# Making 56 modulation tiles during the projections of the mixing sublayers instead of in the 768-token FFNs

## The reference

```python
c_act = jax.nn.silu(c); cc_act = jax.nn.silu(c_ctx)
for layer in range(DEPTH):                                    # DEPTH = 2
    mod   = (c_act @ w_mod[layer] + b_mod[layer])             # 9 vectors of 1024
    mod_c = (cc_act @ w_mod[layer] + b_mod[layer])
    x, xc = hybrid_layer(x, xc, mod, mod_c, ...)
def ffn_sublayer(h, m, sub, ...):                             # shift, scale, gate = 3 of the 9
    y = swiglu(modulate(rms_norm(h, g_pre[sub]), shift, scale), w1, w2)
    return h + MACARON_WEIGHT * gate * rms_norm(y, g_post[sub])
```

## Time and profile before

| | |
|---|---|
| median of 3 runs | 3765.51 us (3759.2 to 3771.49) |
| the profiled execution | 3757.21 us, span 3755.4 us |
| TensorE busy | 3530.5 us, 94% |
| VectorE busy | 2183.8 us, 58% |
| ScalarE, GpSimd busy | 1434.2 us, 721.5 us |
| mean granted TensorE clock | 0.966 |

### The profile page before, as it was taken

The page is one execution under the profiler, slowest core; times in us unless marked ns, Lnnn a source line. Parts: engine busy times, 40 slices in busy tenths (PEclk is TensorE's granted clock), DMA queues, the critical chain, the costliest instruction groups (busy, mean ns, idle before and its releaser), DMA issues.

```text
span 3755.4 us, 52062 instructions
## 1 busy us (share of the span) xinstructions
PE 3530.5 (94%) x19855; PEld 3030.4 (81%) x19855; DVE 2183.8 (58%) x3395; ACT 1434.2 (38%) x2510; POOL 721.5 (19%) x299
## 2 busy tenths in 40 slices
PE   6899999988999999999999898899998999899998
PEld 4899997856789999789999676788878898589656
DVE  6888875167488888788887429421226462541134
ACT  4433333157353333543334317432234423221353
POOL 1111112200211111211111220244442232034202
PEclk9999999999999999999999998999998999799899
DMA  6333332110233332433333220123332222022101
GB/s 227 107 124 123 124 120 86 62 36 1 91 118 116 121 117 97 157 109 116 113 113 119 82 70 17 46 90 100 96 95 68 62 79 68 1 73 90 62 1 56
DMA packets 94531, 333.55 MB, mean 89 GB/s; under 512 B 12272, under 2 KB 14576, under 8 KB 93424
## 3 DMA queue, kind: packets, MB, share of 16 engines
q1 hardware_dynamic: 91248, 316.28, 25.5%
q10 hardware_dynamic: 3072, 14.40, 1.0%
HBM read 322.12 MB, written 8.52 MB: 88 GB/s over the span
## 4 chain that ended last, share of the span: by engine, by line
PE 60%; issue 23%; POOL 6%; DVE 6%; ACT 3%; DMA 2%; SPq 0%; POOLq 0%; DVEq 0%; ACTq 0%
PE psum L2348 21%; PE psum L2227 14%; PE psum L2207 13%; POOL w_parts L668 6%; PE psum L2652 1%; PE psum L2668 1%; PE psum L2262 1%; PE psum L2677 1%; PE psum L2450 1%; PE psum L2121 1%; DMA mod_ring<-modw_dram 1%; PE psum L2424 1%; DVE normed L1302 1%; PE psum L2556 1%; DVE mod_products L1390 0%
## 5 line engine op out<-in xcount | busy, mean ns | idle before, releaser
L668 POOL TENSOR_TENSOR w_parts<-w_raw,w_parts 128x1024 fp32r<-128x1024 f32 x289 | 702.5, 2432 | 2929.2 <-ACT w_parts L708 2916.8
L2207 PE MATMUL psum<-h_parts,w_parts 128*128 128x264 f32 (+1 forms) x5712 | 958.2, 330 | 46.8 <-issue 11.8
L2207 PEld LDWEIGHTS psum<-h_parts,w_parts 128*128 128x128 f32 x5712 | 855.4, 191 | 144.4 <-issue 44.6
L708 ACT ACTIVATE w_parts<-w_raw 128x1024 fp32r<-128x1024 f32 x283 | 300.1, 1061 | 1123.7 <-PE psum L2207 722.5
L2227 PE MATMUL psum<-w_parts,hidden_parts 128*128 128x512 f32 x2904 | 668.3, 391 | 16.5 <-DVE hidden_parts L1262 9.6
L2227 PEld LDWEIGHTS psum<-w_parts,hidden_parts 128*128 128x128 f32 x2904 | 544.6, 188 | 135.6 <-issue 14.6
L2348 PE MATMUL psum<-h_parts,w_parts 128*128 128x384 f32 x2880 | 531.6, 336 | 16.4 <-ACT y_tok L855 14.1
L2348 PEld LDWEIGHTS psum<-h_parts,w_parts 128*128 128x128 f32 x2880 | 505.4, 189 | 20.0 <-issue 17.0
L874 ACT ACTIVATE w_parts<-psum 128x512 fp32r<-128x512 f32 x240 | 143.7, 599 | 367.9 <-PE psum L2348 147.9
L2348 PE MATMUL psum<-h_sums,w_parts 128*128 128x384 f32 x1440 | 268.9, 334 | 0.0
L2348 PEld LDWEIGHTS psum<-h_sums,w_parts 128*128 128x128 f32 x1440 | 251.3, 188 | 0.0
(11 more groups left out here) (352 smaller groups left out, 4121.1 us busy)
## 6 DMA issues: line engine op xcount, KB each, us to landing
w_raw<-wu_dram SPq DMA_DIRECT2D x295, 512.0 KB, 3.6
mod_ring<-modw_dram SPq DMA_DIRECT2D x128, 512.0 KB, 4.4
w_raw_pairs<-wg_dram SPq DMA_DIRECT2D x120, 512.0 KB, 3.7
kept_dram<-resid SPq DMA_DIRECT2D x2, 3136.0 KB, 9.9
resid<-kept_dram SPq DMA_DIRECT2D x16, 392.0 KB, 5.8
na_bias<-rpb_dram ACTq DMA_DIRECT2D x6, 896.0 KB, 4.7
four_dft<-four_dram ACTq DMA_DIRECT2D x2, 2048.0 KB, 8.1
mod_first_k<-modw_dram SPq DMA_DIRECT2D x7, 512.0 KB, 10.0
```

Source lines behind the costliest of these rows:

```text
L668: pool.tensor_tensor(SPL[:, s % 2, 1], RAW[:, s % 2], SPL[:, s % 2, 0].bitcast(F32), ALU.subtract).then_inc(w_split, 1)
L708: act.activation(SPL[:, u % 2, 0], RAW[:, u % 2], ACT.Copy).then_inc(w_hi, 1)
L2207: ins = pe.matmul(PS[:, pair, PSO[a]:PSO[a] + z - a], w[:, wp, k], src[:, xp, k, t0 + a:t0 + z], start=k == 0 and n_ == 0, stop=k == KT - ...
```

## The change

`MOD_PLAN` becomes (2, 2, 1, no boundary tiles) for each fast FFN, 24 tiles each. The mixer of layer 0 makes 32 tiles, that of layer 1 24. After the PSUM copies of each of units 0 to 15 VectorE makes `mix_mods` tiles: two, in layer 1 from unit 8 on one. SP's order in a mixer becomes a written one: the tile loads of step j and then the weights of unit j + 3. The unused product of the first pass goes to a second scratch buffer there. `finish_mods` of the tiles made in a mixer stands before VectorE's rotation. Each tile is still made ahead of its use.

```diff
-MOD_PLAN = [(2, 4, 1, (5, 5, 6, 6)), (2, 2, 1, (4, 4, 4, 4)), (2, 2, 1, (4, 4, 4, 4))]
-MOD_FINISH = [[(0, 16, 64)], [(0, 64, 72), (1, 0, 32)], [(1, 32, 72)]]
+MOD_PLAN = [(2, 2, 1, (0, 0, 0, 0))] * 3
+MOD_RANGE = [(16, 40), (40, 72), (72, 96), (96, 120), (120, 144), (144, 144)]
+MOD_FINISH = [[(0, 16, 40)], [(0, 40, 72)], [(1, 0, 24)], [(1, 24, 48)], [(1, 48, 72)], []]
...
+    JUNK2 = place("mod_products2", [P, D], BF16, a_t + 6144)
...
+    def mix_mods(sub, j):
+        return 2 if sub["T"] == T1 or j < 8 else 1
...
+            def mix_loads(u, sub):
+                tiles = iter(range(*sub["mods"]))
+                w_load(u)
+                sp.wait_ge(erow_ready, sub["in"]["eh"] + 2)
+                for j in range(16):
+                    for _, t in zip(range(mix_mods(sub, j)), tiles):
+                        mod_load(t)
+                    w_load(u + j + 1)
+                w_loads(u + 17, 7)
...
-                elif idx == 1:
-                    w_loads(u, 24)
+                elif sub["kind"] == "mix":
+                    mix_loads(u, sub)
...
@@ ScalarE, mix, before the copies of the Fourier products @@
+                act.wait_ge(mod_used, sub["mods"][1])
...
@@ VectorE, mix, units 0 to 9 @@
                     ins.then_inc(psum_read, 1)
+                    mod_tiles(tiles, mix_mods(sub, j), JUNK2)
...
@@ VectorE, mix, units 10 to 15 @@
                     if j > 10:
                         value_rows(j - 1)
+                    if j < 16:
+                        mod_tiles(tiles, mix_mods(sub, j), JUNK2)
+                dve.wait_ge(mod_used, sub["mods"][1])
+                for done in sub["finish"]:
+                    finish_mods(*done)
```

More of the change, by code:

```diff
@@ L380, in build @@
         sub["fo"] = fast.index(idx) if idx in fast else None
+        sub["mods"], sub["finish"] = MOD_RANGE[idx], MOD_FINISH[idx]
         sub["halves"] = HALVES[T1 if sub["kind"] == "mix" else sub["T"]]
@@ L456, in head_cols @@
         return COLS[0:R, x, i, 8 * g:8 * g + 8].unsqueeze(2).broadcast_to([R, 8, HD])
-    def mod_first_of(fo):
-        return MOD_FIRST + sum(mod_plan_count(x) for x in range(fo))
-    assert mod_first_of(1) == 64 and mod_first_of(2) >= MOD_TILES + MOD_FIRST and mod_first_of(3) == DEPTH * MOD_TILES
+    assert all(mod_plan_count(subs[x]["fo"]) == b_ - a_ for x, (a_, b_) in enumerate(MOD_RANGE[:len(subs)]) if subs[x]["fo"] in (0, 1, 2))
+    assert [a_ for a_, b_ in MOD_RANGE] == [MOD_FIRST] + [b_ for a_, b_ in MOD_RANGE[:-1]] and MOD_RANGE[-1][1] == DEPTH * MOD_TILES
+    def mix_mods(sub, j):
+        return 2 if sub["T"] == T1 or j < 8 else 1
     HT = T1 // 2
@@ L581, in fast_loads @@
                 first, out0, per_pair, per_out = MOD_PLAN[fo]
-                tiles = iter(range(mod_first_of(fo), mod_first_of(fo + 1)))
+                tiles = iter(range(*sub["mods"]))
                 def mods(n):
@@ L1381, in last_half, with mod_half @@
                         y_diag(sub, 0)
-            def mod_half(t, c):
+            def mod_half(t, c, junk=JUNK):
                 d = t - MOD_FIRST
@@ L1388, in mod_half, with mod_tiles @@
                     dve.wait_ge(mod_used, MOD_FIRST + d)
-                dst = JUNK[:] if c == 0 else MODW[:, d % 2]
+                dst = junk[:] if c == 0 else MODW[:, d % 2]
                 return dve.scalar_tensor_tensor(dst, MODW[:, d % 2], 1.0, CBC[:, c], ALU.mult, ALU.mult, accum_out=MODS[:, t, c:c + 1])
-            def mod_tiles(tiles, n):
+            def mod_tiles(tiles, n, junk=JUNK):
                 for _, t in zip(range(n), tiles):
-                    mod_half(t, 0)
-                    mod_half(t, 1).then_inc(mod_used, 1)
+                    mod_half(t, 0, junk)
+                    mod_half(t, 1, junk).then_inc(mod_used, 1)
             def finish_mods(l, t0, t1):
@@ L1508, in fast_ffn @@
                 last_out_units(sub, u, False, 2)
-                dve.wait_ge(mod_used, mod_first_of(fo + 1))
-                for done in MOD_FINISH[fo]:
+                dve.wait_ge(mod_used, sub["mods"][1])
+                for done in sub["finish"]:
                     finish_mods(*done)
```

## The result

The changed kernel takes 3769.34 us (median of 12 runs, 3762.70 to 3773.64) against 3760.98 before (12 runs, 3757.33 to 3771.49): ratio 1.0021, 95% interval 1.0013 to 1.0029, so 5 to 11 us slower and about 8. The forecast was 3774 with a sum of +8.9. The measured slowdown is 0.2%, less than the 0.3% that the prediction set as what can't be told from no change.

The account below looks back on a forecast made before the run. TensorE, busy 94% of the span, was taken as the bound, so only its idle and slow stretches count. FFN gains of 5.95 and 5.1 against mixing-sublayer losses gave +8.9 us, 3774 against the median; range 3758 to 3789.

Parts of the forecast that it names:

- Start of the first FFN: Two tiles instead of four ahead of the first weight sums: TensorE's gap falls from 8.68 to 2.73, 5.95 us gained.
- Boundaries: Between the first FFN's runs, without boundary tiles its stretch falls from 458.9 to 453.8, 5.1 us gained; other FFNs 0.
- Layer 0, middle: Projections, two tiles per unit: copy, tiles and split take 8.3 us against units of 8.32, just fitting; cost 0.
- Layer 0, tail: Unit 15's two tiles delay the last value copy, which the rotary product awaits: 4.9 + 2.4 = 7.3 us lost.
- Layer 0, clock: After the idle stretch ahead of the rotary product TensorE's granted clock is 0.50: 1.6 us lost (0 to 3).
- Layer 1, middle: Short latent-only units let VectorE fall behind; weights of units 9 and 10 come late: 4.6 us lost (0 to 9).
- Layer 1, tail: One tile after the last unit, 2.45 plus a split of 2.4: 4.85 us lost (2.45 to 4.85).
- Clock: Layer 1, after the idle stretch following unit 15: slow granted clock again, 1.6 us lost.
- Entrance: Start of each layer's projections: first tiles and weights come in time; unit 2's split may wait 0 to 1; taken as 0.
- starved loads: Rival: in SP's queue, weight loads behind two ring loads land late in both projections; +20 us, 3785; chance 0.22.
- the relief missing: Rival: pair loads, not tiles, set the first FFN's gap, and only 1.8 us comes back; +18, 3784; chance 0.10.
- The bare tails without a slow clock: Faster rival: splits fit between passes, VectorE keeps pace in layer 1, tails cost 4.9 + 2.45; -4.7, 3761; chance 0.18.

Follow-up runs that it names:

- the kernel with only the gap changed: From the kernel before: two of the first FFN's tiles moved from ahead of its first weight sums to its boundaries (2, 2, then 6 6 6 6); ratio 0.9991.

## Why the prediction held, step by step

- **Start of the first FFN** (-5.95): the gap is 5.99 shorter, right in size, and shown by the kernel with only the gap changed. As a gain it was too large: the first product came 4.25 earlier here, 3.2 to 5.2 in the eight profiles with two tiles. The remark that ScalarE's copy is late next named the last link only: VectorE's tiles hold that one too.
- **Boundaries** (-5.1): -5.18. The other FFNs, put at 0: +0.02 and +1.0, the second within what it varies by.
- **Layer 0, middle** (0): right; with 24, 30 or 32 tiles TensorE does not wait between units 2 and 15; VectorE is behind over the first units and from unit 4 on waits for nearly every unit's end.
- **Layer 0, tail** (7.3): idle +6.26. The mechanism was right, but the split had begun 0.5 us before the pass, so it added 1.68 and not 2.4; the bare tiles are 4.6 (7.31 less 1.68 less 1.05).
- **Layer 0, clock** (1.6): too small. The rotary product is 2.84 longer and the stretch 4.14. Over the profiles the stretch took 327.1 to 328.7 behind the idle tail and 324.6 to 326.3 without it, the kernels whose FFN start was changed left out: about 2.4 on average. I had sized it by 12 short matmuls in the FFN; here the clock came back only after 5 us of work.
- **Layer 1, middle** (4.6): 80.48 - 75.83 = 4.65, though not as two stalls: one of 3.32 at unit 9 (2.7 forecast), none at unit 10, and 1.3 of slow matmuls that the forecast did not have. That the term fits is luck in part. The walk through the queue had 2167.7 for the landing; measured on that clock (FFN 2 ended 3.15 later) it was 2168.3. Turning the order round removed the stall but for 0.62.
- **Layer 1, tail** (4.85): +4.17, of which the split's part is 2.13 (2.4 forecast) and the bare tile's 2.04 (2.45). **Clock** (1.6): the product is 2.06 longer, but the piece behind it no longer than it is elsewhere: 0 in all that can be told.
- **Entrance** (0): a few tenths, inside the forecast 0 to 1. The split of unit 2 waits for a pass, 2.57 long instead of 2.38 in layer 0 and 2.77 instead of 2.34 in layer 1, where TensorE's idle ahead of unit 2 is 11.15 instead of 10.70. The 1.3 to 2.9 that layer 0's 480 matmuls can lose to the clock behind it were not forecast, and what decides them is open.
- **The sum**: +8.9 forecast; -5.99 - 5.18 + 7.28 + 4.14 + 9.27 = +9.5 with the gap for the start, +11.3 with the start's own 4.25, about +8 by the medians. That it comes so close is in part luck: the tails were put 1.7 too high, the start's gain as a whole 1.7 too high in this profile, layer 1's clock 1.6 too high, layer 0's clock 0.8 to 2.5 too low, and layer 0's entrance was left out; these nearly cancel.
- **The signs**: one long pass for nearly every unit came (16 of over 2.5 us in layer 0, one of them 2.74, the rest 2.89 to 3.43), and TensorE waited for the split ahead of unit 9, but not of unit 10. The mixing sublayers grew by 20.7, not under 12.

Of the rivals, starved loads did not come to pass (unit 9's weights took 5.5 to land, not 6.4, and the stall of 3.32 was the only one behind unit 2), nor was the relief missing. The bare tails without a slow clock came only in kernels made for it. On the Trainium skill's SBUF — State Buffer (section SBUF: two separate sides), whose exclusive lock I had weighed as weakly seen: the changed kernel bears it out both ways, in layer 1 for instance:

```profile
2147.84 1.22 DVE L1407 SCALAR_TENSOR_TENSOR mod_products<-mod_ring,cond_rows 128x1024 bf16<-128x1024 f32 x1
...
2148.98 3.41 DVE L1407 SCALAR_TENSOR_TENSOR mod_ring<-mod_ring,cond_rows 128x1024 f32<-128x1024 f32 x1
```
```profile
2148.12 3.19 POOL L684 TENSOR_TENSOR w_parts<-w_raw,w_parts 128x1024 fp32r<-128x1024 f32 x1 [6.08 <-ACT w_parts L724]
```

The split that begins during the first pass takes 3.19 instead of 2.3 to 2.4, and the second pass, which begins during the split, 3.41 instead of 1.22. At the stall of unit 9 the split took 2.34, so TensorE did not wait there for a longer one.

## What to carry to other kernels

Work moved to an engine with spare time was free here except at the end of the stretch, where the next stage waits for that engine's last copy: keep the last unit clear, and give short units less. Where a filler's load waits for its turn, put the loads that the main path needs ahead of it in the queue. And when the profile names an engine as the releaser, look at what stood ahead of that instruction in its queue before calling the wait a floor: here that was worth another 9 us by the ratios, 11 by the medians.

## What was not expected of the hardware

- Idle of 2.77 us ahead of unit 2 was followed by a granted clock of 0.50 in some executions and by 1.00 throughout in one with 2.78 (no tile at unit 15): 480 matmuls of 84.73 to 86.38 us, or of 83.44.
- Keeping TensorE busy with useless multiplications held the clock at 1.00 across a wait of some 7 us and made the next product 3.70 instead of 6.54 us.
